# Forget-gated attention started in the query projection, and norm sums moved from TensorE to VectorE

## The reference

```python
def rmsnorm(x, g):
    y = x * lax.rsqrt(jnp.mean(x * x, axis=-1, keepdims=True) + RMS_EPS)
    return y * g

# layer 1: S5 state space layer, ends in
return h + rmsnorm(y @ w_out, g_post)

# shared keys, values and gates
kvf = rmsnorm(h, g_kv) @ w_kv            # 2048 -> 2 * 2048 + 16
log_f = jax.nn.log_sigmoid(f_logit + b_f)
cum = jnp.cumsum(log_f, axis=1)          # one column for each of 16 heads

# layer 2: FoX
q, z = jnp.split(rmsnorm(h, g_pre) @ w_in, 2, axis=-1)
s = einsum('bhqd,bhkd->bhqk', q_i, k) * scale      # scale = 128 ** -0.5
s = s + c_i[..., :, None] - cum[:, :, None, :]
s = jnp.where(kpos <= qpos, s, NEG_INF)
o = einsum('bhqk,bhkd->bhqd', softmax(s), v)
h = h + rmsnorm((o * jax.nn.silu(z)) @ w_out, g_post)

# layers 3 and 4: retention beside latent attention, each ends in
x = x + gate[:, None, :] * (merged @ w_out)        # then rms_norm of x
```

## Time and profile before

| | |
|---|---|
| median of three runs | 3351.25 us |
| profiled run, of it the span of the trace | 3356.67 us, 3355.0 us |
| PE busy | 3162.6 us, 94% |
| DVE busy | 2236.2 us, 67% |
| ACT busy | 1480.5 us, 44% |
| PE matmuls on `acc`, the two lines L1580 and L1582 with `xs` | 2504.7 and 1956.9 us, overlapping |
| ACT waiting for a block of PE (L469) | 1322.4 us |
| mean of the granted TensorE clock | 0.977 |

### The profile page before, as it was taken

How to read it: one execution, slowest core, us unless ns; L and a number is a source line. 1 busy time by engine, 2 the same in 40 slices (tenths; PEclk the granted TensorE clock), 3 DMA queues, 4 the chain that set the end, 5 groups by cost and what they waited for, 6 DMA issues and landing times. The chain is left out here.

```text
span 3355.0 us, 51764 instructions
## 1 busy us (share of the span) xinstructions
PE 3162.6 (94%) x20984; PEld 2732.0 (81%) x20984; DVE 2236.2 (67%) x2653; ACT 1480.5 (44%) x1843; POOL 108.0 (3%) x206
## 2 busy tenths in 40 slices
PE   6999997999999799999999999989999999999997
PEld 5898886888888688888877788868888887778886
DVE  7687877687565658656766677754755776665564
ACT  5454543334454333345444444433334544444443
POOL 0000000000000000000000000000000000000000
PEclk9999998999999899999999999989999999999999
DMA  5323764777434357645653477644754565335542
GB/s 210 125 105 131 266 249 161 278 252 263 152 119 149 138 207 261 238 155 216 244 204 127 176 264 273 216 182 176 260 179 151 193 252 213 138 140 222 186 170 112
DMA packets 103753, 650.13 MB, mean 194 GB/s; under 512 B 11648, under 2 KB 12800, under 8 KB 39808
## 3 DMA queue, kind: packets, MB, share of 16 engines
q1 hardware_dynamic: 71856, 512.44, 42.6%
q0 software_dynamic: 28528, 105.92, 8.7%
q10 hardware_dynamic: 3168, 28.84, 2.2%
HBM read 632.47 MB, written 14.68 MB: 193 GB/s over the span
## 5 line engine op out<-in xcount | busy, mean ns | idle before, releaser
L1580 PE MATMUL acc<-xs,whi 128*128 128x512 f32 x6960 | 2504.7, 403 | 72.6 <-DVE xs L987 57.9
L1582 PE MATMUL acc<-xs,wlo 128*128 128x256 f32 x6960 | 1956.9, 281 | 0.0
L1580 PEld LDWEIGHTS acc<-xs,whi 128*128 128x128 f32 x6960 | 1316.7, 189 | 404.4 <-issue 55.4
L907 DVE TENSOR_TENSOR wlo<-raw,whi 128x2048 fp32r<-128x2048 f32 x459 | 1051.7, 2291 | 498.0 <-ACT whi L445 497.4
L1582 PEld LDWEIGHTS acc<-xs,wlo 128*128 128x128 f32 x6960 | 1323.3, 190 | 6.1 <-issue 3.4
L445 ACT ACTIVATE whi<-raw 128x2048 fp32r<-128x2048 f32 x459 | 875.1, 1907 | 0.0
L469 ACT ACTIVATE acctmp<-acc 128x256 f32<-128x256 f32 x547 | 208.9, 383 | 1340.9 <-PE acc L1582 1322.4
L957 DVE TENSOR_TENSOR w<-acc,acctmp 128x256 f32<-128x256 f32 (+1 forms) x480 | 205.9, 430 | 460.8 <-ACT acctmp L469 460.2
L929 DVE SCALAR_TENSOR_TENSOR modacc<-modw,cact,modacc 128x1024 f32<-128x1024 f32 x192 | 245.5, 1279 | 12.3 <-DMA modw<-in_modstream 11.0
L424 POOL DMA_DIRECT2D modw<-in_modstream x192 | 101.5, 529 | 2363.0 <-DVE modacc L944 1216.4
L530 ACT ACTIVATE smx<-smx,stat 128x128 f32<-128x128 f32 x96 | 43.0, 448 | 172.5 <-DVE stat L1060 172.5
(11 more groups left out here) (258 smaller groups left out, 2172.3 us busy)
## 6 DMA issues: line engine op xcount, KB each, us to landing
raw<-in_wstream SPq DMA_DIRECT2D x483, 1024.0 KB, 4.8
modw<-in_modstream POOLq DMA_DIRECT2D x192, 512.0 KB, 4.7
residual<-h ACTq DMA_DIRECT2D x2, 2048.0 KB, 6.7
ga_gate<-w ACTq DMA_DIRECT2D x2, 2048.0 KB, 10.3
gated_retention<-w ACTq DMA_DIRECT2D x2, 2048.0 KB, 7.8
h<-gated_retention ACTq DMA_DIRECT2D x2, 2048.0 KB, 9.0
h<-residual ACTq DMA_DIRECT2D x2, 2048.0 KB, 10.1
ga_w<-ga_gate ACTq DMA_DIRECT2D x8, 512.0 KB, 11.0
```

The lines of the kernel that those rows point to most:

```text
L907: dve.tensor_tensor(out=wlo[s % SPL][:, :], in0=raw[s % RAW][:, :], in1=whi[s % SPL][:, :].bitcast(F32), op=ALU.subtract).then_inc(w_lo_do ...
L1580: pe.matmul(acc[par % 2][0:cols, :], whi[w][:, c:c + cols], x_split[:, k, :, :], start=(k == 0), stop=False, skip_group_check=True)
L1582: mm = pe.matmul(acc[par % 2][0:cols, 0:T], wlo[w][:, c:c + cols], x_split[:, k, 0, :], start=False, stop=(k == kts - 1), skip_group_check ...
```

## The change

**1. FoX from q's block 3.** Slot -1 moves behind block 3 of q, and the following ones behind the blocks that follow: slots -1 to 11 lie in q, 12 to 17 in the first six blocks of foxz. For this q is scaled as it is summed (one instruction with a factor on DVE, the same factor in ACT's copy), and the scores wait for their tile of q alone. The cumulative gates enter otherwise: PE turns them once into columns, and DVE adds each head's column as it reads the scores, so that a head's scores take four matmuls, not six; DVE's read of the scores is cut into two. The matmuls behind q's last block (into `bank5`) now wait until ten heads are stored. The gate and split of foxz's output use the same early releases as glu.

**2. Norm sums.** DVE adds the tiles of squares, one per block (`sum_squares`), and PE sums over partitions once at the end (`sum_tiles`). PE's jobs s5out, foxout and out have no side then, so their blocks run in a hardware loop.

**3. Post-norm weights.** ACT multiplies each tile of s5out and foxout by its weight column behind the square; `add_normed` multiplies four tiles at a time by the reciprocal.

**4. Held splits** also at the ends of foxz, s5out, foxout and layer 0's out.

```diff
-RELEASES = [(None, "glu"), (None, "f")] + [...]
+RELEASES = [(None, "glu"), (None, "f"), (None, "foxz")] + [...]
+FOX_FIRST = 3
+def fox_slot_at(job, j):
+    return j - FOX_FIRST - 1 if job == "q" else KT - FOX_FIRST - 1 + j
...
 # ScalarE
-            def square_tile(name, buf, ready, n0):
+            def square_tile(name, buf, ready, n0, weight=None):
                 def side(j):
...
                     act.activation(stg_tiles[:, j % 8, :], buf[:, j, :], ACT.Square).then_inc(sq_done, 1)
+                    if weight:
+                        act.wait_ge(sq_done, SQ_BEFORE[name] + j + 1)
+                        act.activation(buf[:, j, :], buf[:, j, :], ACT.Copy, scale=vcol(weight)(j)).then_inc(sem("post_weighted"), 1)
...
-            project((None, "s5out"), side=square_tile("post0", w3, ...))
+            project((None, "s5out"), side=square_tile("post0", w3, ..., "norm_post0"), held=True)
+            split_held((None, "s5out"))
             root("post0")
...
+                if j >= FOX_FIRST:
+                    attend_slot(0, fox_slot_at("q", j), FOX_H)
             project((None, "q"), side=forget)
-            for g in range(4):
-                act.activation(group(w3)(g), group(w3)(g), ACT.Copy, scale=FOX_SCALE).then_inc(sem("q_scaled"), 1)
-            attend_slot(0, -1, FOX_H)
...
+            def fox_early():
+                z_gate(3, range(3))
+                fox_hi(range(3), (None, "foxz"))
+            project((None, "foxz"), side=before_last(fox_side, fox_early), held=True)
+            z_gate(3, (3,), 1)
+            split_held((None, "foxz"))
             act.wait_ge(acc_done, JOBS[(None, "foxout")][1])
+            fox_hi((3,), None)
...
-                project((l, "out"), side=square_tile(nxt, h, sem("h_updated"), KT * l))
+                project((l, "out"), side=square_tile(nxt, h, sem("h_updated"), KT * l), held=True)
+                if l == 0:
+                    split_held((l, "out"))
 # VectorE
+            def sum_squares(name, j):
+                dve.wait_ge(sq_done, SQ_BEFORE[name] + j + 1)
+                if j == 0:
+                    return
+                if j == 1:
+                    tt(rstd[:, :], stg_tiles[:, 0, :], stg_tiles[:, 1, :], ALU.add).then_inc(sq_used, 2)
+                    return
+                dve.wait_ge(sq_used, SQ_BEFORE[name] + j)
+                tt(rstd[:, :], rstd[:, :], stg_tiles[:, j % 8, :], ALU.add).then_inc(sq_used, 1)
...
+                    if g < 4:
+                        dve.wait_ge(sem("post_weighted"), KT * total + 4 * g + 4)
+                        tt(group(src)(g), group(src)(g), bcast(rstd[:, :], 4), ALU.mult).then_inc(sem("post_scaled"), 1)
...
             rms("post0")
             dve.wait_ge(sem("x_back"), 16)
-            add_normed(w3, vcol("norm_post0"), 0)
+            add_normed(w3, 0)
+            split_held((None, "s5out"))
 # TensorE
-            def sum_tile(name, j):
-                pe.wait_ge(sq_done, SQ_BEFORE[name] + j + 1)
-                pe.matmul(bank[0][:, 0:T], part[:, :], stg_tiles[:, j % 8, :], start=(j == 0), stop=(j == KT - 1), ...)
+            def sum_tiles(name):
+                pe.wait_ge(sq_used, SQ_BEFORE[name] + KT)
+                pe.matmul(bank[0][:, 0:T], part[:, :], rstd[:, :], start=True, stop=True).then_inc(sem("tiles_summed"), 1)
...
             def fox_scores(i, b):
                 sel = ident[:, i:i + 1]
+                pe.wait_ge(acc_summed, JOBS[(None, "q")][1] + i + 1)
                 for n, (lo, m) in enumerate(((0, P), (P, T))):
                     o = b[:, lo:lo + m]
                     pe.matmul(o, w3[:, i, n * P:(n + 1) * P], w1[:, i, 0:m], start=True, stop=False)
-                    pe.matmul(o, fcum[:, 2, n * P:(n + 1) * P], sel.to_broadcast([P, m]), start=False, stop=False)
                     mm = pe.matmul(o, sel.to_broadcast([P, P]), fcum[:, 4, 0:m], start=False, stop=True)
...
+            project((None, "q"), xs, fresh="pre1", side=q_side,
+                    before_mod=(sem("att_stored"), fox_slot_at("q", KT - 1) - 1))
```

More of the change, by code:

```diff
@@ L113 @@
 NSQUARES = {n: k for n, k, _ in NORMS}
-RELEASES = [(None, "glu"), (None, "f")] + [(l, n) for l in range(2) for n in ("gb3", "retproj", "mlaproj")]
+TILE_NORMS = [n for n, k, _ in NORMS if k == KT]
+RELEASES = [(None, "glu"), (None, "f"), (None, "foxz")] + [(l, n) for l in range(2) for n in ("gb3", "retproj", "mlaproj")]
 OVER = {n: f for n, _, f in NORMS}
 SPLIT_GROUPS = dict(SPLITS)
+FOX_FIRST = 3
+FOX_SILU = 5
+def fox_slot_at(job, j):
+    return j - FOX_FIRST - 1 if job == "q" else KT - FOX_FIRST - 1 + j
 ROPE_L = 8 + 1 + 2 * MLA_G
@@ L752, in z_gate @@
-            def z_gate(g):
-                act.wait_ge(acc_summed, JOBS[(None, "foxz")][1] + 4 * g + 4)
+            def z_gate(g, tiles=range(4), turn=0):
+                first = 4 * g + tiles[0]
+                act.wait_ge(acc_summed, JOBS[(None, "foxz")][1] + 4 * g + tiles[-1] + 1)
                 if g:
-                    act.wait_ge(sem("silu_used"), g)
-                act.activation(zsig[:, :, :], group(w1)(g), ACT.Sigmoid).then_inc(sem("silu_gate"), 1)
+                    act.wait_ge(sem("silu_used"), g + turn)
+                act.activation(zsig[:, tiles[0]:tiles[-1] + 1, :], w1[:, first:first + len(tiles), :], ACT.Sigmoid
+                               ).then_inc(sem("silu_gate"), 1)
@@ L946, in one @@
                 def one(j, s):
-                    if mod is not None and not (held and j == nb - 1):
+                    if mod is not None and not (held and j == nb - 1 and key in RELEASES):
                         mod_step(mod, j, s)
@@ L1055, in attend_slot @@
                         dve.wait_ge(sem("att_turned"), a - 1)
-                    link(dve.scalar_tensor_tensor(out=smx[:, i % 2, :], in0=bank[i % 2][:, 0:384], scalar=scale,
-                                                  in1=mask[:, kind, :], op0=ALU.mult, op1=ALU.add))
+                    if shift:
+                        for n, (lo, hi) in enumerate(((0, 128), (128, 384))):
+                            last = dve.scalar_tensor_tensor(out=smx[:, i % 2, lo:hi], in0=bank[i % 2][:, lo:hi], scalar=shift(n, i),
+                                                            in1=mask[:, kind, lo:hi], op0=ALU.add, op1=ALU.add)
+                        link(last)
+                    else:
+                        link(dve.scalar_tensor_tensor(out=smx[:, i % 2, :], in0=bank[i % 2][:, 0:384], scalar=scale,
+                                                      in1=mask[:, kind, :], op0=ALU.mult, op1=ALU.add))
                     dve.reduce_max(stat[:, i % 2, 0:1], smx[:, i % 2, 0:128], AXX)
@@ L1351, in _ @@
             project((None, "q"), lambda j: tile(w3, j), side=forget)
-            dve.wait_ge(sem("masks_loaded"), 16)
             def silu_mul(base, g, z, gate, x):
```

156 lines of the change are left out of this document (94 added, 62 removed).

## The result

The changed kernel takes 3311.93 us (median of 4 runs, 3310.22 to 3315.15); the kernel before took 3353.12 in the same session (3349.46 to 3359.76). The ratio is 0.9876, with an interval of 0.9858 to 0.9894: 41 us less. The forecast was 3310 us. The profiled run took 3310.22 us, its span is 3308.5; the span before was 3355.0. The two profiles are 46.5 us apart, 5 more than the medians.

What follows compares the result with a forecast made beforehand. PE's own order of work, plus where it stands still, was taken as the bound. 21.6 + 10.7 - 0.3 + 0.6 + 5.2 + 1.4 + 2.2 - 0.45 = 41.0 us off 3351.25 forecast 3310 us, range 3298 to 3322.

Steps and rivals of the forecast that it cites:

- Squares: s5out, foxout, both outs: removing the matmul behind each block shortens 56 periods by 0.385 us each, 21.6 us (18.5 to 24.6).
- VectorE at nothing: Four norm jobs: DVE's added sum of squares costs nothing, with 4.6 of 5.6 us filled in s5out; uncovered, up to 24 us.
- rival (a): Four norm jobs: VectorE sets the period, so the 21.6 us gain is lost and the kernel takes 3332 us; chance 0.08.
- rival (b): Attention slots in q run in series, each waiting for DVE and ACT: 58 us lost, 3368 us in all; chance 0.03.
- rival (d): Only the job changes around foxz fail; their 5.8 us gain becomes a loss of some 3, 3319 us; chance 0.08.
- Scores: FoX slots: two score matmuls fewer per head save 0.67 us each, 10.7 us over 16 heads, less 0.3 for turning gates.
- the two turns of the gates: FoX: PE's added turning of the cumulative gates into columns costs some 0.3 us with what it interrupts.
- q to foxz: Job change: PE's wait for scaled q becomes one for head 9's store; distance 16.64 becomes 16.4 us, gain 0.6.
- foxz to foxout: Job change: extras fall from 11.7 to 6.5 us with glu's order of the end; gain 5.2 us (4 to 6.5).
- Norms: Norm ends: s5out and foxout gain 1.4 us together, layer 0's out 2.2; the last norm loses 0.45.
- The table (rival c): Three norms: a flush beside ACT's table load adds about 1.3 us each, 3314 us in all; chance 0.03.
- The sum: Whole kernel: all terms together save 41.0 us, from a median of 3351.25 us to 3310 us.

Runs made afterwards that it cites:

- the added row: One more DVE add of 1024 columns, result unused, in blocks 1 to 14 of s5out, foxout and both outs, against the changed kernel; 3316.96 us, 0.9881.
- the repeat: The changed kernel run once more with no edit, beside its variants; 3313.89 us, ratio 0.9894 to the kernel before.

## Why the prediction was right, and where it was off

- **Squares, 21.6 us (18.5 to 24.6).** The periods fell from 5.98 to 5.65 in three jobs and to 5.55 in one: 42 x 0.33 + 14 x 0.43 = 19.9 us. Right, and shown by putting the matmul back, which brings 5.98 back in all four jobs. Taking the middle of the two levels was a fair guess, since the level changes between jobs for no reason that the runs show.
- **VectorE at nothing.** Right, with more room than was counted. The count of 4.6 us was 4.61 by the rows, and the pause that was called forced gave way. So rival (a) falls by the periods of 5.65 and by the added row; rival (b) by q's periods of 8.06 to 8.16, in which ACT waits for PE and PE has no wait at all; rival (d) by the two job changes below, which both gained.
- **Scores, 10.7 - 0.3 us.** From q's first row to foxout's 16.5 us were saved. The two job changes below take 7.7 of them (without foxout's first period, which lies behind), and 8.8 are left where 10.4 were forecast. The price of the matmuls was right: putting them back costs 11.3 us. The term that was too small is the 0.3 us for the two turns of the gates. It counted them as work of PE alone; PE also waits 2.13 us there for DVE's gates (1.93 in the repeat), and the block grows by 2.05 us. 10.7 - 2.05 is 8.65.
- **q to foxz, 0.6 us.** The store ended 7.0 us behind acctmp (6.95 forecast), and from it to the next acctmp went 8.8 us where ga to rg had 9.46. The distance was 15.77, not 16.4: a gain of 1.3. The mechanism, one wait in the place of another, is shown by moving the chunk. Its tail was mis-sized by 0.7 us, in the share that depends on how soon the clock returns.
- **foxz to foxout, 5.2 us.** Two pauses, as said, and 10.86 us where about 12 were named, 0.7 of them for the next block. In this profile foxout's first block (7.50 us) took more than the 0.7 assumed: together 10.86 - 5.65 + 1.85 = 7.1 us of extras, not 6.5, a gain of 4.6. In the repeat the same sum is 10.74 - 5.65 + 0.80 = 5.9, a gain of 5.8. The term was right within this scatter.
- **Norms.** The root at s5out came 5.15 us behind acctmp (5.2 forecast) and at out 4.92 (5.0), bound by ACT as said. s5out and foxout gave 0.4 and 0.9 (1.4 forecast in all), out 2.8 (2.2). The last norm cost 1.0 us in this profile and not 0.45. But the add is not what the term missed, as PE's sum over partitions shows. In the changed kernel, with the window around it (granted clock third from the end of the line):

```profile
3291.38 1.22 PE L1687 MATMUL bank<-rstd,part 128*128 128x256 f32 x2 [2.36 <-DVE rstd L1097]
```
```profile
3291.00:3293.00 2.00, 1.22 (x2) 0.50 (x2) 0.61 (x2) 1.17 (x1) 0.00 (x0) 0.56 0.00 0
```

  And in the version with the chunk in foxout, which has the same instructions here:

```profile
3286.03 0.70 PE L1687 MATMUL bank<-rstd,part 128*128 128x256 f32 x2 [2.36 <-DVE rstd L1097]
```

  The wait is the same, but in the first the granted clock is 0.56 and the sum takes 1.22 us. In the second it takes 0.70, and the end comes 18.95 us behind the last acctmp where it was 18.49 before: 0.46, as forecast. Of the twelve profiles with DVE's sum, eight have 0.70 us and an end at 18.94 to 19.01, the others 0.94 to 1.22 us and an end up to 19.48. The forecast's 0.45 holds at the full clock and has no part for the slow one.
- **The table (rival c).** The root starts 1.30 us behind its table's load in s5out and in the version with the root first, on the path both times. The Trainium skill (ScalarE: Activation LUTs, What ACT_TABLE_LOAD costs) adds a drain of about 1.38 us to each load; these rows don't show it, and the rival falls. Nor does it lie ahead of the load, which starts within 0.02 us of the end of ACT's row before it, each time in the changed kernel.
- **The sum, 41.0 us.** The stages of the change gave 38.4 in the profile, 2.6 less than the terms: 1.7 in the squares, as three of the four norm jobs stood at 5.65, and 1.75 in the turns of the gates, while the other differences add up to 0.8 the other way. In the repeat they gave 42.9. The untouched stages gave another 8.0, mostly through their levels. The medians are 41.2 apart. That they fall on the forecast within a us is luck in part; what the traces and experiments bear out is each term within some 2 us.

## What to carry over

Before a matmul's cost is taken from its columns, look at what it does to the stream around it: a single-column fp32 matmul between pairs of another type cost 0.34 us, 256 columns 0.43, each against the pairs beside it. Where a stage's product of another stream ends a job, ask whose buffer its result shares: a bank shared with the heads' outputs cost 7 to 8 us per job change. Moving the product to a job whose end waits anyway cost nothing that could be seen at foxout, and 0.9 us at layer 0's out. Where work moves to an earlier place, ask also when its inputs are ready: the turn of the gates, 0.3 us of work, waited 2.1 us. And where a plain block has two levels without a known cause, judge an edit of a few us by its stage, not by the total.

## What was not expected of the hardware

- A plain block of 16 matmul pairs takes 5.55 or 5.65 us (pairs 0.347 or 0.353 us apart) under the same instructions and the same granted clock of 1.00, mostly for a whole job. With the fp32 matmul of squares behind each block, all eight jobs seen (four before, four with the sums put back) stood at the low level plus 0.43 (their pairs lie 0.347 us apart); with the tiny one all four stood at 5.65 + 0.34 (pairs 0.353 apart). No reason was found.
- The Trainium skill (FP8 and Floating Point Precision, TensorE Precision Notes) has true fp32 as four passes through the array. A pass of 256 columns in the blocks' type takes some 0.115 us here, from the start of `wlo`'s matmul to that of the next `whi`'s. Four of them make an estimate of 0.46 us for 256 columns of fp32, and the 0.43 us measured are near it. For one column the same estimate gives almost nothing, and the run shows 0.34 us; there the measurement decides.
- After a stall of 4.67 us the granted clock was 0.70 over the 8 us behind it; after two pauses (2.03 and 2.64 us in the changed kernel) the granted clock was 0.52 and 0.62 in the next 4 us there, and foxout's first block lasted 6.3 to 7.5 us in place of 5.65, differently from run to run. The last norm lost 0.5 us to it in one profile and nothing in another.
